# Earlier PSUM evacuation, sinks on VectorE and spread output tiles in the second block's attention

## The reference, cut to what matters

```python
# sliding half ("A"): 128 keys back, a sink per head, a position bias
s = jnp.where(allowed, q @ k.T * 64 ** -0.5 + bias, NEG)
m = jnp.maximum(s.max(axis=-1), sink)
e = jnp.exp(s - m[..., None])
pr = e / (e.sum(axis=-1, keepdims=True) + jnp.exp(sink - m)[..., None])
o_a = pr @ v
# sparse half ("B"): latent keys c_kv, the top 256 keys of an index score
s = jnp.where(valid, q_abs @ c_sel.T * scale + bias, NEG)
o_b = jax.nn.softmax(s, axis=-1) @ c_sel @ w_uv
# both
mixed = gate_a * (o_a @ w_branch_a) + gate_b * (o_b @ w_branch_b)
h = h + mixed @ w_out
```

## Time and profile before

| | |
|---|---|
| median of three executions | 1626.81 us |
| the profiled execution, its own time | 1627.97 us |
| its span, first to last instruction | 1626.2 us |
| mean granted clock of TensorE | 0.977 |
| PE busy | 1541.2 us, 95% of the span |
| DVE, ACT, POOL busy | 819.6, 618.4, 396.6 us |
| chain that ended last, share on PE | 88% |

### The profile page before, as it was taken

The page is one execution under the profiler, slowest core; times in us unless marked ns, Lnnn a source line. Parts: engine busy times, 40 slices in busy tenths (PEclk is TensorE's granted clock), DMA queues, the critical chain, the costliest instruction groups (busy, mean ns, idle before and its releaser), DMA issues.

```text
span 1626.2 us, 19536 instructions
## 1 busy us (share of the span) xinstructions
PE 1541.2 (95%) x7198; PEld 1223.9 (75%) x7202; DVE 819.6 (50%) x1612; ACT 618.4 (38%) x1118; POOL 396.6 (24%) x380
## 2 busy tenths in 40 slices
PE   6899989999999999999999999878999999999995
PEld 5688665688878888888887788645677888888884
DVE  5537566444354343433446786565563543443444
ACT  5423467423244232322445434544443321222222
POOL 3200655200020000000037544555641210220112
PEclk9999999999999999999999999978999999999998
DMA  5743200333232323233322833112322333333321
GB/s 188 132 107 96 100 1 14 116 93 102 78 104 84 98 91 102 93 98 97 96 80 66 217 132 126 53 46 78 129 79 78 99 95 96 99 95 100 92 83 58
DMA packets 46670, 154.11 MB, mean 95 GB/s; under 512 B 5699, under 2 KB 5891, under 8 KB 46577
## 3 DMA queue, kind: packets, MB, share of 16 engines
q1 hardware_dynamic: 41840, 137.63, 26.9%
q0 software_dynamic: 4736, 15.25, 4.4%
HBM read 142.78 MB, written 9.55 MB: 94 GB/s over the span
## 4 chain that ended last, share of the span: by engine, by line
PE 88%; DVE 6%; ACT 3%; issue 2%; DMA 1%; DVEq 0%; SPq 0%; another core or an unknown queue 0%; ACTq 0%
PE PSA L577 86%; PE PSA L782 1%; ACT AR L1300 1%; PE PSA L926 1%; DVE WL L1695 1%; DMA WR<-w_in 1%; DVE AHL L1898 1%; DVE AR L1785 0%; DVE AR L1810 0%; ACT WH L1228 0%; DVE AR L1783 0%; DVE ARR L1939 0%; DVE AR L2368 0%; DVE AR L2275 0%; ACT Bh L1381 0%
## 5 line engine op out<-in xcount | busy, mean ns | idle before, releaser
L577 PE MATMUL PSA<-Ah,WH 128*128 128x512 f32 x1072 | 425.0, 396 | 19.0 <-DVE WL L1695 19.0
L577 PE MATMUL PSA<-Ah,WL 128*128 128x512 f32 x1072 | 420.5, 392 | 0.0
L577 PE MATMUL PSA<-Al,WH 128*128 128x512 f32 x1072 | 420.4, 392 | 0.0
L1228 ACT CAST WH<-WR 128x1024 fp32r<-128x1024 f32 (+3 forms) x234 | 240.7, 1030 | 226.1 <-PE PSA L577 222.3
L1695 DVE TENSOR_TENSOR WL<-WR,WH 128x1024 fp32r<-128x1024 f32 (+3 forms) x207 | 252.4, 1219 | 81.4 <-ACT WH L1228 81.1
L577 PEld LDWEIGHTS PSA<-Ah,WH 128*128 128x128 f32 x1072 | 203.4, 190 | 64.6 <-issue 22.5
L577 PE MATMUL PSA<-Bh,WH 128*128 128x512 f32 (+1 forms) x592 | 231.8, 392 | 11.7 <-DVE ARR L1939 5.6
L577 PEld LDWEIGHTS PSA<-Ah,WL 128*128 128x128 f32 x1072 | 203.0, 189 | 42.9
L577 PEld LDWEIGHTS PSA<-Al,WH 128*128 128x128 f32 x1072 | 203.1, 189 | 42.9 <-issue 0.7
L577 PE MATMUL PSA<-Bh,WL 128*128 128x512 f32 (+1 forms) x592 | 230.0, 389 | 0.0
L577 PE MATMUL PSA<-Bl,WH 128*128 128x512 f32 (+1 forms) x584 | 227.4, 389 | 0.0
(11 more groups left out here) (363 smaller groups left out, 1983.0 us busy)
## 6 DMA issues: line engine op xcount, KB each, us to landing
WR<-w_in SPq DMA_DIRECT2D x228, 512.0 KB, 3.5
gt_tmp<-AR SPq DMA_DIRECT2D x16, 256.0 KB, 2.2
WR<-w_in SPq DMA_DIRECT2D x8, 384.0 KB, 3.1
XT<-scr_tmp POOLq DMA_DIRECT2D x8, 264.0 KB, 10.4
XT<-xT_in SPq DMA_DIRECT2D x4, 512.0 KB, 9.3
XT<-scr_tmp POOLq DMA_DIRECT2D x8, 256.0 KB, 15.5
XT<-xT_in POOLq DMA_DIRECT2D x1, 2048.0 KB, 9.6
x_tmp<-XT POOLq DMA_DIRECT2D x1, 2048.0 KB, 7.5
```

The costliest lines, as they stand in the source:

```text
L577: return pe.matmul(o, l, r, start=start, stop=stop)
L1228: ac.copy(WH[p][:, 0:n], WR[j % RAW][:, 0:n]).then_inc(w_hi, 1)
```

## The change

Four things are moved or replaced; the number of matmuls stays as it is.

1. ACT evacuates a projection piece in the piece's own step (before: one step later), DVE takes the low half one step after it (before: three).
2. The sink of an A unit is copied by DVE, one 128 x 1 copy in front of the maxima of each of the 32 units. The 16 copies of POOL and the semaphore for them are gone; ACT no longer waits for it.
3. The output tiles of the sliding half go to steps 46, 55, 63, 64, 65, 66, 67 and 71 (before: 46, 49, 56, 63, 64, 65, 67 and 68), three of them in bank 7 and then one each in banks 1, 3, 0, 2, 7 (before four in bank 7 and then 1, 3, 0, 2). Gates, products and waits follow.
4. The weight splits of these tiles go to other steps, and DVE does its part two steps behind ACT (before: in the same step). The scaling of gate 5 goes behind POOL's loop.

```diff
-        A_AT = {46: 0, 49: 1, 56: 2, 63: 3, 64: 4, 65: 5, 67: 6, 68: 7}
+        A_AT = {46: 0, 55: 1, 63: 2, 64: 3, 65: 4, 66: 5, 67: 6, 71: 7}
         B_AT = {70: 0, 72: 1, 74: 2, 75: 3}
-        A_BANK, B_BANK = (7, 7, 7, 7, 1, 3, 0, 2), (1, 3, 0, 2, 4, 5, 7, 6)
-        SCALE_AT = {41: 0, 43: 1, 49: 2, 56: 3, 58: 4, 60: 5}
-        TANH_AT = {45: (0,), 48: (1,), 55: (2,), 62: (3,), 63: (4,), 64: (5,), 66: (6,), 67: (7,), 70: (8,), 71: (9,), 72: (10,),
+        A_BANK, B_BANK = (7, 7, 7, 1, 3, 0, 2, 7), (1, 3, 0, 2, 4, 5, 7, 6)
+        SCALE_AT = {41: 0, 50: 1, 56: 2, 58: 3, 60: 4}
+        TANH_AT = {45: (0,), 54: (1,), 62: (2,), 63: (3,), 64: (4,), 65: (5,), 67: (6,), 68: (7,), 70: (8,), 71: (9,), 72: (10,),
                    73: (11,), 77: (12, 13, 14, 15)}
-        GATED_AT = {48: 0, 51: 1, 58: 2, 65: 3, 66: 4, 67: 5, 69: 6, 70: 7}
-        SPLIT_AT = {26: ("br2a", 0), 29: ("br2a", 1), 34: ("br2a", 2), 53: ("br2a", 3), 65: ("br2b", 0), 67: ("br2b", 1),
-                    70: ("br2b", 2)}
+        GATED_AT = {48: 0, 57: 1, 65: 2, 66: 3, 67: 4, 68: 5, 69: 6, 73: 7}
+        SPLIT_AT = {36: ("br2a", 0), 43: ("br2a", 1), 51: ("br2a", 2), 57: ("br2a", 3), 65: ("br2b", 0), 68: ("br2b", 1),
+                    73: ("br2b", 2)}
...
-                if o < 4:
-                    pe.wait_ge(r_mc, (5, 5, 6, 7)[o])
-                    if o == 1:
-                        pe.wait_ge(m_dv.sem, m_dv.at("a", 0))
+                if A_BANK[o] == 7:
+                    pe.wait_ge(r_mc, 5 + min(o, 3))
                 else:
-                    pe.wait_ge(r_mx, 57 + o)
+                    pe.wait_ge(r_mx, 58 + o)
...
-                    if o < 4:
-                        pe.wait_ge(m_dv.sem, m_dv.at("a", 4 + o))
-                    if o == 6:
-                        pe.wait_ge(r_mc, 8)
+                    if o < 4 or o == 6:
+                        pe.wait_ge(m_dv.sem, m_dv.at("a", 3 + o if o < 4 else 7))
...
                         pe.wait_ge(r_mc, pair)
-                        pe.wait_ge(m_dv.sem, m_dv.at("a", pair - 4))
+                        pe.wait_ge(m_dv.sem, m_dv.at("a", pair - 5))
...
                 ac.wait_ge(r_mx, i + 1)
-                if x == "A":
-                    ac.wait_ge(r_sk, i // 2 + 1)
...
-                    if t - 1 in PROJ_AT:
-                        projected(t - 1)
+                    if t in PROJ_AT:
+                        projected(t)
...
+                if x == "A":
+                    dv.tensor_copy(E2[x][c][:, n:n + 1], NSK[:, h:h + 1])
...
-                    if t - 3 in PROJ_AT:
-                        projected(t - 3)
+                    if t - 1 in PROJ_AT:
+                        projected(t - 1)
...
-                    if t in SPLIT_AT:
-                        split_to(tid[SPLIT_AT[t]])
+                    if t - 2 in SPLIT_AT:
+                        split_to(tid[SPLIT_AT[t - 2]])
...
-            def sinks(i):
-                x, h, qt, n, meta = unit2(i)
-                c, s = ((2688, 264), (5856, 976), (7104, 272), (7648, 272))[i % 8 // 2]
-                if i > 7:
-                    pl.wait_ge(r_tr, i - 6)
-                pl.tensor_copy(AHL[:, c + n:c + n + s + 1:s], NSK[:, h:h + 2]).then_inc(r_sk, 1)
...
-            for q in range(6, 16):
+            for q in range(len(SCALE_AT), 16):
                 scale2(q)
```

More of the change, by code:

```diff
@@ L342, in build @@
         h_z, h_vm = sem("h_z"), sem("h_vm")
-        r_sc, r_mx, r_sk, r_ex, r_rc, r_nm = sem("r_sc"), sem("r_mx"), sem("r_sk"), sem("r_ex"), sem("r_rc"), sem("r_nm")
+        r_sc, r_mx, r_ex, r_rc, r_nm = sem("r_sc"), sem("r_mx"), sem("r_ex"), sem("r_rc"), sem("r_nm")
         r_tr, r_cd, r_ca, r_pv = sem("r_tr"), sem("r_cd"), sem("r_ca"), sem("r_pv")
@@ L2522, in scale2 @@
                 pl.tensor_tensor(G2[q % 8], G2[q % 8], RBG[2], ALU.mult).then_inc(g_sc.sem, 1)
-            pl.wait_ge(r_ns, 1)
-            sinks(0)
             for i in range(U2):
                 x, h, qt, n, meta = unit2(i)
-                if i % 2 == 0 and i < 30:
-                    sinks(i + 2)
                 if i in (26, 28):
```

## The result

The changed kernel took 1610.63 us (median of four runs, 1608.6 to 1613.71), the kernel before 1629.13 us on the same chip (four runs, 1625.9 to 1632.57): a ratio of 0.9888, 95% interval 0.9858 to 0.9918. That is 18.5 us less, where 13 were forecast. The profiled execution took 1613.71 us; its span is 1611.9 us, 14.3 us shorter than before's.

The account below looks back on a forecast made before the run. PE, busy 95%, was taken as the bound, with gains only where it idles or runs at the lower clock. Gains of 6.0, 2.5, 1.5, 3.6, 2.2 less costs of 0.3, 1.8, 1.0 gave 13 us: 1613.8 us, range 1603 to 1621.

Parts of the forecast that it names:

- the likeliest case: Whole change: its parts sum to about 13 us faster, 1613.8 us for the median; chance 0.42.
- pieces: Units 5 to 20: earlier evacuation cuts the ring of PE and DVE waits; 6.0 us gained (1 to 7.9).
- split of t = 29: Weight split at step 29: DVE's 1.15 us stand for ACT and 1.23 us work go; 2.5 us gained.
- sinks: DVE's sink copies, 0.08 to 0.1 us each; 0.3 us lost on the 16 units outside the ring.
- split of t = 34 against 38: Weight split moved from step 34 to 38: DVE's 1.54 us stand goes; 1.5 us gained (0 to 2.8).
- tile of t = 49: Output tile waiting 1.45 us for its bank moves to step 55; 3.6 us gained there, DVE's 0.95 us stand included.
- tile of t = 56: Output tile mostly at 1.2 GHz moves behind the last scores, among tiles at 2.4 GHz; 2.2 us gained (0 to 4).
- The rival in which DVE is the bound of half A: Sliding half: dearer sinks and semaphore delay cut the pieces' gain to 1.2 us; 8 us faster, 1619; chance 0.20.
- the rival in which the clock comes back: Two stretches of 11 and 15 us return to 2.4 GHz as gaps shrink; 21 us faster, 1606; chance 0.18.
- no effect: PE's wait for the piece becomes other waits of equal length, splits cost the same on new steps; 1625; chance 0.06.
- gates late: Tail: gates 14 and 15 arrive at about 1186, ACT blocks some 4 us; 9 us faster, 1618; chance 0.10.
- clock lost: Half B, steps 32 to 62: TensorE stays at 1.2 GHz where two tiles leave; plus 25 us, 1639; chance 0.04.

Follow-up runs that it names:

- pieces alone: Kernel before with only the earlier evacuation of projection pieces on ACT and DVE; ratio 0.9916 to before.
- sinks alone: Kernel before with only the sink copies moved from POOL to DVE; ratio 0.9997 to before.
- tables alone: Kernel before with only the new output-tile steps, banks, waits and two-step weight splits, pieces and sinks as before; ratio 0.9913 to before.
- three copies: Kernel after with two more 128x1 DVE copies per sink, to unused columns; ratio 0.9883 to before.
- sinks gone: Kernel after with the sink copies back on POOL; ratio 0.9865 to before, and 0.986 when run again.
- the low half's stand gone: Kernel after with sinks back on POOL and DVE's low half of the first six pairs one step later; 1605.3 us, ratio 0.983 to before.
- the kernel with its splits in one step: Kernel after with DVE's half of each weight split in ACT's own step instead of two steps behind; ratio 0.9936 to before.
- the lag alone: Kernel before with only DVE's half of each weight split moved two steps behind ACT's; ratio 0.9938 to before.
- The kernel after, again: Kernel after, unchanged, timed again beside the kernel with sinks back on POOL; ratio 0.9902 to before.

## Why the prediction was right, and where its terms were off

The forecast was 1613.8 us, the time 1610.63: the mechanism of the likeliest case held, and the time lies inside its range of 1609 to 1619. Of the signs named for it, PE's wait for the low half is at 0.5 us, units 5 to 20 take 21.2 us, DVE's waits for ACT's half of a split are gone up to M63, the tile at t = 55 starts after 0.28 us, the tile at t = 63 runs at the full clock, and ACT's last four gates have no idle time ahead of them. None of the signs against it came. The profiled difference by stretch, after less before, against the terms of the sum put to their stretches (0–5 has none, and took 0.24 us more):

| stretch | terms | forecast | measured |
|---|---|---|---|
| 5–21 | pieces | −6.0 | −7.45 |
| 21–32 | split of t = 29, sinks | −2.2 | −2.52 |
| 32–45 | split of t = 34 against 38 | −1.5 | −2.48 |
| 45–56 | tile of t = 49, stand, split of t = 45 | −2.4 | −4.84 |
| 56–63 | tile of t = 56, split of t = 59, ACT | −3.4 | −4.03 |
| behind M63 | one tile more | +2.75 | +3.42 |

*Pieces.* The round was worked out as 2.65 us a pair: it is 21.24 / 8 = 2.66 in the kernel after, 2.55 with pieces alone. The sum took 6.0 of the 6.8 us that this gives, a caution that the runs did not need. Between profiles with nothing at 1.2 GHz in 5–21 the pieces are worth 6.9 us (sinks alone, 28.14, to the kernel after, 21.24) and 7.4 (tables alone, 27.75, to pieces alone, 20.39); what the row "before" shows beyond that goes with its 3.4 us at the lower clock.

*Sinks.* The price from start to start was well judged (0.06 us in most units, 0.08 on the mean of all 32; forecast 0.08 to 0.1), and so was the part in the ring: 2.65 us a pair had 0.1 for the sink in it, and the runs show 2.66 with the sinks on DVE and 2.55 without. Mis-sized was the 0.3 us for the units behind the ring, put so low because PE had been full there: 21–32 loses 0.3, 1.1 and 1.5 us in three pairs of kernels, a difference that goes with the clock. With both, the sinks on DVE cost 1.2 to 2.4 us and gain nothing, so this part of the change was a small loss. The rival in which DVE is the bound of half A is right in so far as, with the ring cut, what is put on DVE or taken from it moves 5–21 (three copies +1.34, sinks gone −0.8, the low half's stand gone a further −1.8). Its price of 4.8 us in the first term was not reached, and where it counts 24 more instructions on DVE in this stretch, the edit adds one to each of the 16 units.

*Weight splits.* The stand of DVE for ACT was the right reason and the largest under-estimate. All stands together were put at 3.6 us (1.15, 1.54 and 0.95) with 1.23 us of work moved around them. Two steps between the halves are worth 5.3 us on the kernel before and 8.9 us on the kernel after. A stand is dearer than its own length where it delays maxima, with them ACT, then the low half of a pair and then an output tile on PE, as in the rows of the kernel with its splits in one step; how the 5.3 us divide between such delays and the clock is not shown.

*Output tiles.* No run moves the tiles without moving the steps of the splits, so what follows holds for the new tables as a whole. They bring nothing in total without the lag (208.38 against 208.23 us): 2.0 us are gained in 21–32 and 1.3 in 56–63, and 2.3 are paid behind M63 and 1.4 between. On top of the lag, on the kernel before, they bring 7.2 us (211.80 to 204.64), of which 2.0 lie in 5–21, where neither acts, so about 5. In 45–56 the kernel before took 26.81 us, with the lag alone 24.53, with the new tables alone beside pieces and sinks 27.38, with both 21.95 to 21.98. So the sum was wrong in adding up the two: the places pay only where DVE does not stand in them. Of t = 56's tile, 3.0 of the 4.0 us that 56–63 lost came with the lag alone, without moving it. Its term had the move as what takes the tile out of the lower clock; the lag does that by itself, so the total of 56–63 came out near the forecast partly for another reason than the one given.

*The tail and the gates.* As worked out. Tile and gates cost 2.48 us up to the last low half (2.75 forecast), POOL waited 2.00 us for the last gates where it had waited 3.20, and PE's gap is the same. The 0.94 us behind go with a stretch of 3.4 us at 1.2 GHz from 1169.0; no other of the profiles has one there, and all the others have 61.50 to 61.54.

*The clock.* The fall from 34 us at 1.2 GHz to 20 is the direction of the rival in which the clock comes back. But both stretches named there are still at 0.76 and 0.77. With pieces, tables and low half changed and no sinks on DVE it does come back: 7 us are left and the attention is 8 us below that of the kernel after. How much of this is the clock and how much the waits themselves, no run separates. The rivals "no effect", "gates late" and "clock lost" fell.

The gap between 18.5 us of medians and 14.3 of spans is mostly in the time ahead of M0, 3.4 us longer in this profile, with 37 us at 1.2 GHz in place of 24 and the same instructions. The profiled execution is also the slowest of its four. The attention's own difference, 17.7 us, leaves this out, but it leans on the one profile of the kernel before. The kernel with the sinks alone, which is as slow as that one, has 213.76 us in the attention with 10 us less at 1.2 GHz; from there the difference is 14.3 us, and the sum had 12.7. From either, 45–56 is the stretch that was most under-sized (4.8 and 5.1 us against 2.4). The kernel after, again, had 1616.9 us, ratio 0.9902 [0.9883, 0.9921].

## What to carry to other kernels

In a pipeline of engines that each run in order, look for an instruction that needs the result another engine makes in the same step: put it one or two steps later, and do this before moving larger work around, since here the move without it gave nothing. Cut first the wait that closes a ring (two engines that wait for each other in turn), and then count small instructions again: what was free on an engine with room is paid for once the ring is gone (here 0.8 us for 16 copies). Judge such an edit by the stretch it is in, since 0.8 us that repeats there is not seen in a total that varies by several us. And before two profiles are compared, add up their time at the lower clock in each stretch, the unchanged ones too: here the start of the attention moved with it by up to 6.9 us.

## What the hardware showed unexpectedly

A copy of 128 x 1 on DVE, by line in the kernel after (ns min/median/max, first and last start), and the two copies added by the experiment with three:

```profile
L1895 DVE COPY AHL<-AR x32: 125/142/155, 1030.0 to 1069.7; 128x1 f32<-128x1 f32 x32
```

```profile
L1896 DVE COPY AR<-AR x64: 129/143/155, 1030.3 to 1071.9; 128x1 f32<-128x1 f32 x64
```

It is 0.142 us long, but in 26 of the 32 units the maxima behind it start 0.05 to 0.07 us after it starts (in the other six 0.17): successive instructions overlap, and the length by itself overstates the cost, on the mean of 0.08 us by nearly two times. The fixed cost of each instruction on SBUF operands that the Trainium skill gives ("VectorE: DVE Perf Modes", the section on the TRN2 errata) agrees with the length, not with the distance of starts.

A subtraction of 128 x 1024 on DVE took 1.21 to 1.25 us in all rows above but two, and 2.18 and 2.22 in these, both of the kernel with its splits in one step. Beside both POOL scaled a gate, as its timeline shows:

```profile
1120.78 1.27 POOL L2513 TENSOR_TENSOR AHL<-AHL,AR 128x512 f32<-128x512 f32 x1
...
1135.31 1.27 POOL L2513 TENSOR_TENSOR AHL<-AHL,AR 128x512 f32<-128x512 f32 x1
```

The Trainium skill has the two engines' access to SBUF as shared, with contention for DVE instructions that read two SBUF operands ("GPSIMD Engine Reference", Specifications), and this subtraction reads two; the trace agrees, with the figures that follow. All 14 profiles together settle more than these two rows. DVE does 2898 subtractions for weight splits in them, and the 2320 with no POOL instruction beside them took 1.23 us at most. In 41 cases a TENSOR_TENSOR of POOL had started 0.1 to 0.8 us before the subtraction: all 41 took 1.60 to 2.32 us, and each ended 1.08 to 1.09 us after POOL's instruction, as if it had stood until that one was done. A further 27 had 0.24 us or less of POOL's instruction ahead of them and took 1.21 to 1.32 us, and one took 1.41 us beside a scaling of probabilities on POOL. In the 387 cases in which DVE had started first, none took over 1.23 us; POOL's instruction of 128 x 512, 1.26 to 1.31 us with DVE idle beside it, took 2.2 us in 280 of them. So whichever of the two starts first keeps its pace and the other pays. No run changed POOL's work by itself, so this is read from the order of starts, which decides all 428 of those cases.
